# LayerNorm's weight and bias applied after the transposition, on ScalarE, and the first two row tiles of h1 turned around the middle of a product

## The reference

```python
m = jax.nn.sigmoid(g_a) * y_a + jax.nn.sigmoid(g_b) * y_b
h = layer_norm(DEEPNORM_ALPHA * h + m @ w_out[l], ln1_g[l], ln1_b[l])
f = jnp.square(jax.nn.relu(h @ w_ff1[l])) @ w_ff2[l]
h = layer_norm(DEEPNORM_ALPHA * h + f, ln2_g[l], ln2_b[l])
```

## Time and profile before

| | |
|---|---|
| median of 3 runs | 1056.41 us (1055.19 to 1056.47) |
| time of the profiled execution | 1055.34 us |
| its span, first to last instruction | 1053.5 us |
| mean granted clock of TensorE over the span | 0.997 |
| busy: PE / PEld | 1037.4 us (98%) / 900.4 us (85%) |
| busy: DVE / ACT / POOL | 817.4 us (78%) / 547.2 us (52%) / 100.2 us (10%) |
| chain that ended last, by engine | PE 94%, DVE 3%, ACT 1% |

### The profile page before, as it was taken

The page is one execution under the profiler, slowest core; times in us unless marked ns, Lnnn a source line. Parts: engine busy times, 40 slices in busy tenths (PEclk is TensorE's granted clock), DMA queues, the critical chain, the costliest instruction groups (busy, mean ns, idle before and its releaser), DMA issues.

```text
span 1053.5 us, 13902 instructions
## 1 busy us (share of the span) xinstructions
PE 1037.4 (98%) x5644; PEld 900.4 (85%) x5644; DVE 817.4 (78%) x931; ACT 547.2 (52%) x638; POOL 100.2 (10%) x112
## 2 busy tenths in 40 slices
PE   9999999999999999999999999997999999999997
PEld 8788888888888888888888888886999999888885
DVE  5778878678966788878877545899887776897997
ACT  6576653454444645354436534543656656655560
POOL 1301000000012010001101001122000000220200
PEclk9999999999999999999999999999999999999999
DMA  9847322223973665322323314871232333999862
GB/s 318 242 115 161 98 80 80 91 81 129 220 163 112 194 126 164 110 91 90 113 67 120 100 48 154 169 229 40 70 92 81 122 119 123 183 206 248 177 223 80
DMA packets 97647, 143.02 MB, mean 136 GB/s; under 512 B 5196, under 2 KB 59852, under 8 KB 97456
## 3 DMA queue, kind: packets, MB, share of 16 engines
q1 hardware_dynamic: 77280, 96.38, 27.9%
q0 software_dynamic: 20016, 45.62, 21.5%
q10 hardware_dynamic: 288, 0.13, 0.1%
HBM read 137.40 MB, written 4.73 MB: 135 GB/s over the span
## 4 chain that ended last, share of the span: by engine, by line
PE 94%; DVE 3%; ACT 1%; issue 1%; DMA 1%; SPq 0%; DVEq 0%
PE bank L648 30%; PE bank L650 29%; PE bank L649 29%; PE bank L769 2%; PE bank L964 1%; PE bank L888 1%; PE bank L1013 1%; DVE w_lo L1909 1%; DMA w_raw<-in_w_mem_kv 1%; PE bank L988 0%; ACT w_hi L1638 0%; PE bank L821 0%; PE bank L820 0%; ACT m_left_hi L1649 0%; DVE residual L2714 0%
## 5 line engine op out<-in xcount | busy, mean ns | idle before, releaser
L1909 DVE TENSOR_TENSOR w_lo<-w_raw,w_hi 128x2048 fp32r<-128x2048 f32 (+2 forms) x78 | 167.8, 2153 | 86.6 <-ACT w_hi L1296 65.2
L648 PE MATMUL bank<-act_t_hi,w_hi 128*128 128x512 f32 (+1 forms) x592 | 226.5, 383 | 5.2 <-DVE act_t_lo L1909 5.2
L650 PE MATMUL bank<-act_t_hi,w_lo 128*128 128x512 f32 (+1 forms) x592 | 224.3, 379 | 0.0
L649 PE MATMUL bank<-act_t_lo,w_hi 128*128 128x512 f32 (+1 forms) x592 | 224.2, 379 | 0.0
L648 PEld LDWEIGHTS bank<-act_t_hi,w_hi 128*128 128x128 f32 x592 | 112.1, 189 | 25.4 <-issue 5.4
L650 PEld LDWEIGHTS bank<-act_t_hi,w_lo 128*128 128x128 f32 x592 | 111.9, 189 | 20.9
L649 PEld LDWEIGHTS bank<-act_t_lo,w_hi 128*128 128x128 f32 x592 | 112.1, 189 | 19.9
L1296 ACT ACTIVATE w_hi<-w_raw 128x2048 fp32r<-128x2048 f32 (+1 forms) x44 | 81.4, 1850 | 19.4 <-PE bank L650 19.4
L648 PE MATMUL bank<-w_hi,hidden_hi 128*128 128x512 f32 x216 | 84.1, 389 | 0.0
L650 PE MATMUL bank<-w_hi,hidden_lo 128*128 128x512 f32 x216 | 84.0, 389 | 0.0
L649 PE MATMUL bank<-w_lo,hidden_hi 128*128 128x512 f32 x216 | 84.0, 389 | 0.0
(11 more groups left out here) (468 smaller groups left out, 2361.9 us busy)
## 6 DMA issues: line engine op xcount, KB each, us to landing
w_raw<-in_w_in SPq DMA_DIRECT2D x38, 1024.0 KB, 5.2
w_raw<-in_w_ff POOLq DMA_DIRECT2D x16, 1024.0 KB, 15.1
w_raw<-in_w_ff SPq DMA_DIRECT2D x28, 512.0 KB, 4.9
w_raw<-in_w_ff SPq DMA_DIRECT2D x13, 1024.0 KB, 8.1
w_vo_sums<-in_w_in POOLq DMA_DIRECT2D x8, 1024.0 KB, 9.0
w_out_sums<-in_w_out POOLq DMA_DIRECT2D x8, 1024.0 KB, 9.3
w_vo_sums<-in_w_in SPq DMA_DIRECT2D x6, 1024.0 KB, 5.3
w_raw<-in_w_out SPq DMA_DIRECT2D x5, 1024.0 KB, 6.3
```

Source lines behind the costliest of these rows:

```text
L648: pe.matmul(dst, lh, rh, start=start, stop=False, skip_group_check=onto)
L649: pe.matmul(dst, lh, rl, start=False, stop=False, skip_group_check=onto)
L650: return pe.matmul(dst, ll, rh, start=False, stop=stop, skip_group_check=onto)
L1909: return dve.tensor_tensor(dst, src, hi.bitcast(f32), ALU.subtract)
```

## The change

- g and b of the first LayerNorm come in as 16 more columns of `vector_columns` (one value for each partition and chunk) and are applied behind the turn, where a column of h1 is a partition: ACT does the four chunks of bank 6 (`h1_rows_hi`), DVE the four chunks of bank 7 (`h1_right_chunks`), each chunk 128 x 128. `TH` is then copied from `H1T`.
- Before the turn only `(x - mean) * rstd` is made, in one pass on ACT (`h1_normed`), from rstd and minus mean times rstd; POOL makes the latter in one more small instruction.
- For the residual, DVE multiplies each tile of `RES` by g inside the loop over the `w_ff1` products (`h1_times_g`), and POOL adds b with four accumulating DMAs. `L1B` is no longer loaded.
- Statistics are split in half rows and stand at other places of DVE's list.
- The buffers of P6's and P7's right operands are exchanged, and their order; the first `w_ff1` block goes into the buffer that P3 used, and its low part is subtracted by DVE, not by POOL.
- PE turns tile 0 between the halves of P7 and tile 1 behind P7, ahead of P4. Tile 2 is turned after 33 matmuls of the pair, tile 3 after 30 more.

```diff
-        OTHER_SLOT = {WO + 2: 3, WO + 3: 2, Q: 1, ff1_0: 2}
+        OTHER_SLOT = {WO + 2: 3, WO + 3: 2, Q: 1, ff1_0: 4}
...
-        WO2_RIGHT = (P1, P3, P5, P2, P7, P6, P4)
+        WO2_RIGHT = (P1, P3, P5, P2, P6, P7, P4)
...
-        WO2_SLOT = {P1: 0, P5: 1, P3: 2, P2: 3, P7: 4, P6: 0, P4: 3}
+        WO2_SLOT = {P1: 0, P5: 1, P3: 2, P2: 3, P6: 4, P7: 0, P4: 3}
...
 PE
-                for i in (P1, P2, P5, P6, P3, P7):
+                for i in (P1, P2, P5, P6, P3):
                     wo2_product(i)
-                wo2_product(P4, lambda: turn_row("h1T", h1_done, 0))
+                wo2_product(P7, lambda: turn_row("h1T", h1_done, 0))
                 turn_row("h1T", h1_done, 1)
+                wo2_product(P4)
...
-            ff1_pair_by_halves({(0, 1, 3): 2, (1, 0, 3): 3})
+            ff1_pair_by_halves({(0, 1, 2): 2, (1, 0, 4): 3})
...
 ACT
                 wo2_left_hi_of(P2)
-                wo2_right_hi(P7)
                 wo2_left_hi_of(P5)
                 wo2_right_hi(P6)
+                wo2_right_hi(P7)
                 wo2_left_hi_of(P6)
                 wo2_left_hi_of(P3)
+                wo2_right_hi(P4)
                 wo2_left_hi_of(P7)
                 wo2_left_hi_of(P4)
-                wo2_right_hi(P4)
-                act.wait_ge(*wo2_done[P6])
+                act.wait_ge(*wo2_done[P3])
                 split(ff1_0)
+                h1_normed(0)
+                h1_normed(1)
+                h1_rows_hi(0)
+                h1_rows_hi(1)
                 act.wait_ge(w2_loaded, 16)
                 act.activation(W2H[:, :], W2[:, :], ACT.Copy).then_inc(w2_hi, 1)
...
+                h1_normed(2)
+                h1_rows_hi(2)
+                h1_normed(3)
+                up_hi_of(0)
+                h1_rows_hi(3)
+
+            def h1_normed(j):
+
+                act.wait_ge(centered, j + 1)
+                act.activation(RES[:, j, :], RES[:, j, :], ACT.Identity, bias=NMR[:, j:j + 1],
+                               scale=RST[:, j:j + 1]).then_inc(h1_done, 1)
+
+            def h1_rows_hi(j):
+
+                b = full(act, ("h1T", j, 0))
+                for c in range(4):
+                    ins = act.activation(H1T[:, c, tile_of(j)], b[:, tile_of(c)], ACT.Identity, bias=col(C_L1B + c), scale=col(C_L1G + c))
+                free(ins, ("h1T", j, 0))
                 for half in range(2):
...
+                    drained(act, ("h1T", j, half))
+                    c = slice(4 * half, 4 * half + 4)
+                    act.activation(TH[:, c, tile_of(j)], H1T[:, c, tile_of(j)], ACT.Copy).then_inc(h1_hi, 1)
...
+            act.wait_ge(*block_done[ff1_0])
             left_sum_hi(SAH[0][:, :, :], turned(H1T, 0, 0), 3)
...
 DVE
+            def h1_right_chunks(j):
+
+                b = full(dve, ("h1T", j, 1))
+                for c in range(4):
+                    ins = dve.tensor_scalar(H1T[:, 4 + c, tile_of(j)], b[:, tile_of(c)], col(C_L1G + 4 + c), col(C_L1B + 4 + c),
+                                            ALU.mult, ALU.add)
+                free(ins, ("h1T", j, 1))
...
                 wo2_left_lo_of(P2)
                 wo2_left_lo_of(P5)
+                wo2_right_lo(P6)
                 wo2_m_sum(P6)
+                wo2_left_lo_of(P6)
                 wo2_right_lo(P7)
-                wo2_right_lo(P6)
-                wo2_left_lo_of(P6)
...
                 for t in range(2): wo2_last_fold(P2, t)
+                wo2_right_lo(P4)
                 wo2_left_lo_of(P7)
+                for t in range(2): wo2_part_fold(P6, t)
+                for t in range(2): row_stats(t, 0)
                 wo2_left_lo_of(P4)
...
+                for t in range(2):
+                    wo2_last_fold(P3, t)
+                    row_stats(t, 1)
+                for t in range(2): wo2_part_fold(P7, t)
+                dve.wait_ge(w_hi, ff1_0 + 1)
+                lower(WL[4][:, :], RAW[0][:, :], WH[4][:, :]).then_inc(own_lo, 1)
+                h1_right_chunks(0)
+                for t in range(2): row_stats(2 + t, 1)
+                wo2_last_fold(P4, 0)
+                row_stats(2, 0)
+                h1_right_chunks(1)
                 h1_rows_lo(0)
+                h1_rows_lo(1)
+                wo2_last_fold(P4, 1)
+                row_stats(3, 0)
                 dve.wait_ge(w2_hi, 1)
                 lower(W2L[:, :], W2[:, :], W2H[:, :]).then_inc(w2_lo, 1)
...
+                h1_right_chunks(2)
                 h1_rows_lo(2)
+                h1_right_chunks(3)
                 up_lo_of(0)
                 h1_rows_lo(3)
...
+                if i == P1 and 2 <= q < 2 + TT: h1_times_g(q - 2)
...
 POOL
-            load_all(L1B[:, :], a["ln1_b_2"][0], ln_in)
             add_w_out2(0, 1, 0, P6)
-            split_own(ff1_0)
             for j in range(TT):
                 pool.wait_ge(ln_var, TT + j + 1)
                 rstd(RST[:, j:j + 1], MV[:, j, 1:2], 1, 1.0, LN_EPS)
+                pool.wait_ge(rstd_done, roots[0])
+                pool.tensor_scalar(NMR[:, j:j + 1], MV[:, j, 0:1], RST[:, j:j + 1], -1.0, ALU.mult, ALU.mult).then_inc(centered, 1)
+            for j in range(TT):
+                pool.wait_ge(h1_done, TT + j + 1)
+                pool.dma_start(RES[:, j, :], a["ln1_b_2"][0].partition_broadcast(P), accum_op=ALU.add).then_inc(ln_in, 16)
```

More of the change, by code:

```diff
@@ L151, in two_blocks @@
     ROWS = place("reversed_rows", [P, 1], mybir.dt.uint32)
-    VC = place("vector_columns_sb", [P, P + 2 + H])
+    VC = place("vector_columns_sb", [P, P + 2 + H + 2 * KC])
     THIN_RAW = place("thin_w_raw", [P, KC, THIN])
@@ L167, in two_blocks @@
     FLOOR = place("den_floor", [P, TT, H])
+    RDEN_PLACE = top[0]
     RDEN = place("den", [P, TT])
+    NMR = at("minus_mean_times_rstd", [P, TT], RDEN_PLACE)
     SMX_PLACE = top[0]
@@ L282, in two_blocks @@
     L1G = at("ln1_g_all", [P, D], A + 72 * K1)
-    L1B = at("ln1_b_all", [P, D], A + 76 * K1)
     F1 = at("ff_hidden", [P, 8, 2048], A + 16 * K1)
@@ L288, in two_blocks @@
     OL = [WL[2], at("w_out2_lo1", [P, 2048], A + 80 * K1, f32r), at("w_out2_lo2", [P, 2048], XS + 16 * K1, f32r), WL[0], WL[1]]
+    WH.append(OH[2])
+    WL.append(OL[2])
     OLEFT = (XS, TURNED, TURNED + 8 * K1, TURNED + 16 * K1, XS + 24 * K1, A + 24 * K1)
@@ L325, in two_blocks @@
     C_B2, C_B2G, C_GN, C_LOW, C_BG, C_GATE2 = 64, 64 + 40, 64 + 56, P, P + 1, P + 2
+    C_L1G, C_L1B = P + 2 + H, P + 2 + H + KC
     def col(c):
@@ L341, in two_blocks @@
         w0_hi, w0_lo = sem("w_block0_first_quarter_and_second_half_hi"), sem("w_block0_to_4_early_parts_lo")
-        own_lo = sem("w_lo_done_by_gpsimd")
+        own_lo = sem("w_lo_of_first_ff1_block")
         quad_raw = [sem(f"w_quadrants{s}_loaded") for s in range(QUADS)]
@@ L1634, in wo2_right_hi @@
                 if i == P2: act.wait_ge(*block_done[ff1_0 - 2])
-                if i == P7: act.wait_ge(*block_done[ff1_0 - 1])
-                if i == P6: act.wait_ge(*wo2_done[P1])
+                if i == P6: act.wait_ge(*block_done[ff1_0 - 1])
+                if i == P7: act.wait_ge(*wo2_done[P1])
                 if i == P4: act.wait_ge(*wo2_done[P2])
@@ L1675, in w_out2_operands @@
                 for half in range(2):
-                    key, c = ("h1T", TT - 1, half), slice(4 * half, 4 * half + 4)
-                    act.wait_ge(h1_lo, 2 * TT - 1 + half)
-                    free(act.activation(H1T[:, c, tile_of(TT - 1)], quarters(bank[6 + half][:, :]), ACT.Copy), key)
+                    drained(act, ("h1T", j, half))
+                    c = slice(4 * half, 4 * half + 4)
+                    act.activation(TH[:, c, tile_of(j)], H1T[:, c, tile_of(j)], ACT.Copy).then_inc(h1_hi, 1)
@@ L2587, in h1_rows_lo, with row_stats, h1_times_g @@
                     c = slice(4 * half, 4 * half + 4)
+                    drained(dve, ("h1T", j, half))
                     dve.wait_ge(h1_hi, 2 * j + half + 1)
[L2589 to L2611, removed]
+                    lower(TL[:, c, tile_of(j)], H1T[:, c, tile_of(j)], TH[:, c, tile_of(j)]).then_inc(h1_lo, 1)
+            def row_stats(j, half):
+                if j >= 2 and half == 1: dve.wait_ge(vo_added, WO2_ADDS + WO2_PART[P7] + j - 1)
+                ins = half_stats(RES, j, half)
+                if half == (1 if j < 2 else 0):
+                    link(ins)
+                    mean_var(j).then_inc(ln_var, 1)
+            def h1_times_g(j):
+                if j == 0: dve.wait_ge(ln_in, 16)
+                full(dve, ("h1T", j, 1))
+                dve.tensor_tensor(RES[:, j, :], RES[:, j, :], L1G[:, :], ALU.mult).then_inc(h1_done, 1)
             def up_sums(g):
@@ L2929, in left_sums @@
                     drained(dve, ("h1T", TT - 1, half))
+                dve.wait_ge(h1_lo, 2 * TT)
                 dve.tensor_tensor(a22, a21, a22, ALU.add).then_inc(left_sum, 1)
@@ L2993, in fold_one @@
                 b = full(dve, key)
+                dve.wait_ge(ln_in, 16 * (1 + TT))
```

(7 more changed lines are left out.)

19 lines of the change are left out of this document (removed).

## The result

The changed kernel takes 1066.6 us (median of 5, 1062.5 to 1066.7) against 1056.4: ratio 1.0086, interval 1.0070 to 1.0103. It is slower, as forecast, but by some 10 us instead of 3.1, and outside the stated range. Its profiled execution took 1063.7 us with a span of 1061.8, 8.3 more than the span before.

A forecast was written before the change was run, and what follows sets the result against it. PE, busy 98% of the span, was taken as the bound, with DVE's chain and PE's queue fixing the end. P5 3.1 us later gave 1055.34 + 3.1 = 1058.4, so 1059.5 us for the median; range 1056.8 to 1062.5.

The forecast's parts named there:

- Row tile 0 up to its turn: Tile 0's statistics, POOL's small instructions and ACT's norm: PE can turn at 712.65, after a new pause of about 3.4 us.
- rival (b): POOL's small instructions before tile 0's turn take 1.28 us here too: +2.2 us, 1061.7; chance 0.06.
- Row tile 1, bank 7: In tile 1's turn PE waits for DVE's chunks to free bank 7, 716.8 to 720.5: second new pause, 3.7 us.
- The joint, tiles 2 and 3, DVE's chain: From the pair's start at 728.7 through two turns and DVE's sums to P5 at 758.6, not 755.50: +3.1 us.
- The shift of P5: P5 of the first w_ff1 product moves +3.1 us; taken as the end's shift, since PE has no long pause behind it.
- the sum: Whole kernel: 1055.34 + 3.1 = 1058.4 us for that execution, 1059.5 for the median.
- rival (a): TensorE's clock falls in PE's new pauses: one fall gives 1060.9 us, two 1062.3; chance 0.18.
- The inner range: Whole kernel: the case's own range, 1058.2 to 1060.9 us, from chunk price bounds of -1.6 to +1.1.
- The sign: Whole kernel: slower, chance 0.70, because the order adds waits although DVE has less to do.
- (c): DVE is early, tile 0's aggregate ends at 707.6: end +0.6 us, 1057.0; chance 0.20 with small errors of its kind.
- (d): DVE's amount of work decides, not its waits: P5 7.8 us sooner, -4.7, 1051.7; chance 0.10.
- 3.2 us less to do: DVE's work: 9.6 us of passes removed, 2.2 of subtraction and 4.2 of chunks added, 3.2 us less.

The follow-up runs named there:

- e4: Changed kernel with PE turning tile 0 behind P7 and tile 1 between the halves of P4, each half a product later: 1052.4 us, ratio 0.9968.
- e2: Changed kernel with DVE doing tile 0's right chunks (bank 7) ahead of the fold of P7's second half: 1058.3 us, ratio 1.0019.
- e1: Changed kernel with idle matmuls (results unused) filling three PE pauses, 14, 15 and 9 of them: 1060.3 us, ratio 1.0034.
- e7: e4 with ACT's left chunks of tile 0 ahead of tile 1's norm, and P5's low part ahead of two DVE instructions: 1053.3 us, ratio 0.9975.
- a1: The changed kernel as it is, measured again on the chip of e1, e2 and e4: 1065.9 us, ratio 1.0083.
- e8: e7 with 8 idle matmuls in the pause of 2.0 us ahead of the pair: 1052.3 us, ratio 0.9963.
- e9: e4 with only the low part for P5 moved ahead, ACT's order kept: 1052.0 us, ratio 0.9962.
- e3: Changed kernel with PE's turns at their places of before, tile 0 between P4's halves, tile 1 behind P4: 1055.8 us, ratio 1.0001.
- e6: Changed kernel with the first w_ff1 low part subtracted by POOL behind tile 1's rstd, not by DVE: 1060.7 us, ratio 1.0042.

## Why the prediction was wrong

- **Row tile 0 up to its turn: right.** 712.65 forecast, 712.83 measured. POOL's three instructions took about what the prediction had for them; below them stand the same instruction for tile 2 and DVE's work beside it:

```profile
710.29 0.19 POOL L3119 TENSOR_SCALAR rstd_tmp<-mean_var 128x1 f32<-128x1 f32 x1 [20.37 <-DVE mean_var L2456]
710.56 0.57 POOL L3120 TENSOR_TENSOR rstd<-rstd_tmp,minus_half 128x1 f32<-128x1 f32 x1
711.23 0.27 POOL L3218 TENSOR_SCALAR minus_mean_times_rstd<-mean_var,rstd 128x1 f32<-128x1 f32 x1
...
729.97 2.68 POOL L3218 TENSOR_SCALAR minus_mean_times_rstd<-mean_var,rstd 128x1 f32<-128x1 f32 x1
```

```profile
730.11 2.49 DVE L1928 TENSOR_TENSOR act_t_lo<-h_t,act_t_hi 128x512 fp32r<-128x512 f32 x4
```

  For tile 2 it took 2.68 us, beside DVE's low parts with two SBUF operands, and PE didn't wait for that tile. So rival (b) didn't come where it would have counted in the changed kernel; in e4 it did.
- **Row tile 1, bank 7: right.** A second pause of 3.7 us forecast, 3.83 measured; e2 removes it by the order alone.
- **The joint, tiles 2 and 3, DVE's chain: right at full clock.** With the falls in these pauses taken away (e1) the pair starts at 728.6 (728.7 forecast), P5 at 758.7 (758.6) and the median is 1060.3 (1059.5). The shift of P5 is the shift of the end as the prediction took it, unless a fall follows P5: the profiled execution of e1 has one, its span grew by 4.7 us for a P5 3.2 later; e1's two executions with the highest clock took 1058.4, which is the 1058.4 of the sum.
- **The step that failed is rival (a).** The sum let PE come back from each pause at full clock, which puts the clock at nothing; the fall got a chance of 0.18, with two falls at most. In the first profile it fell at all three new pauses ahead of the `w_ff1` products: from the turn of tile 0 to DVE's fold at 718.01 it took 5.2 us instead of 3.9, from bank 7's release to the fold at 727.30 5.1 instead of 3.55, and the pair's first 33 matmuls 5.5 instead of 4.0. These 4.4 us, and 0.7 of small errors (four chunks on DVE took 1.28, not 1.05), are the difference between 758.6 and 763.69. The price of 1.4 for a fall was about right (1.3 to 1.6); their number was not. My argument "each pause is shorter than the one seen" took one observation for a limit. The row of before showed that a fall can come after 5.2 us, and not that it can't after 3.4; e7 shows one after 2.0.
- **The range.** Its upper end was the case of two falls on top of the sum. By the medians of a1 and e1 the clock costs 5.6 us (1065.9 less 1060.3), about four times 1.4; the first profile has three falls and lies 2.9 us under its median, a1's has four, one of them long. The inner range has a slip: 1059.5 with 1.6 below and 1.1 above is 1057.9 to 1060.6, not 1058.2 to 1060.9. It changes nothing, as both lie far below the result.
- **Sign and rivals (c), (d).** The sign was right for its reason: the waits are there at full clock too (e1, ratio 1.0034). DVE wasn't early, and its amount of work didn't decide. From 679 us to the end of the low part for P5 DVE is busy 66.4 us against 70.2, yet the kernel got slower, and e4, with the same work in another order, is faster than before by 3.4 to 4 us. The prediction's "3.2 us less to do" also leaves out the four multiplications by g, which it names elsewhere; over the whole kernel DVE is busy 818.2 us against 817.4. For (d) the condition "PE need not wait for bank 7" holds in e2 and e4. In e4 most of its gain came; e2 stayed 2 us slower than before, so the condition alone was not enough: the place of the turns had to change with it.

## What to carry to other kernels

When a step on PE is moved ahead, write down for each wait of the step when its data is ready, its output buffers included: here the transposes waited for a bank that another engine drains far down its list. Price every pause of PE twice, once as a wait and once as a possible stretch at half clock behind it, since the length of a wait alone did not tell in these runs whether a fall would follow. Several short waits may be better than one long, which e7's spread beside e8 and e9 hints at but the overlapping medians don't show. Where a pause can't be removed, matmuls nobody reads keep the clock up (2.3 us in the kernel before, 5.6 in the changed one). And a wait removed close to the end of a chain, as the one before P5, can be given back at once behind it.

## What the runs showed of the hardware

- The clock fell to its lower level at waits of 3.42, 3.83 and 2.14 us in the change's first profile, of 3.42 and 2.52 in e2, of 3.69 and 2.09 in e3, of 2.16 and 2.09 in e6, of 1.99 in e7, of 2.09 (before P5) in e1 and at all four waits of a1 (3.43, 3.83, 2.12, 2.09). It did not fall at waits of 3.48 and 1.62 in e6, of 2.08 and 2.09 before P5 in the change's first profile and in e2, nor at 0.69, 1.28, 0.60 and 2.09 in e4.
- In a1 the low stretch began over 1 us after PE had resumed, with the transposes behind the wait still at full speed.
- The same kernel differs by this between executions: 1063.1 to 1067.1 us for the change, 1052.1 to 1053.8 for e4. Why one pause has a fall behind it and another of the same length has none stays open.
- A POOL instruction on one column took 0.27 us beside DVE's statistics, and 2.68 and 2.39 us beside DVE's low parts, which read two SBUF operands.
